# The readout laid into the end of the recurrence, output product and norms by token halves, up projection begun by halves

## The reference

```
hx = modulate(rmsnorm(x, pre_mix_g), sh1, sc1)                 # 1024 tokens; hc likewise, 256 context tokens
q, k, v, o, gates = split(hx @ m_in_w + m_in_b)                # 4 heads, dk 128, dv 256
hxf = chunk_scan(q, k, v, gates_f, state_f)                    # chunks of 128 tokens, first to last
hxb = chunk_scan(reversed q, k, v, gates_b, state_b)           # last to first
h   = hxf + hxb
hn  = h * rsqrt(mean(h*h over each head's 256) + eps) * norm_g
y   = (hn * sigmoid(o)) @ m_out_w                              # the output product
x   = x + g1 * rmsnorm(y, post_mix_g)                          # first norm
hx  = modulate(rmsnorm(x, pre_ffn_g), sh2, sc2)                # second norm
u, g = split(hx @ up_w)                                        # the up projection, 2 x 2816 columns
x   = x + g2 * rmsnorm((silu(dwconv3(g)) * u) @ down_w, post_ffn_g)
```

## Time and profile before

| | |
|---|---|
| timed runs | 2344.55 us median of 3 (2343.93 to 2348.63) |
| profiled execution | 2347.46 us, its span 2345.6 us |
| PE busy | 2157.1 us (92%), 9876 instructions |
| DVE, ACT, POOL busy | 1103.7 (47%), 774.6 (33%), 671.8 (29%) |
| DMA | 245.19 MB, mean 105 GB/s; the SP queue 234.75 MB, 32.5% of 16 engines |
| chain that ended last | PE 41%, issue 38%, DVE 10%, POOL 6% |

### The profile page before, as it was taken

The page is one execution under the profiler, slowest core; times in us unless marked ns, Lnnn a source line. Parts: engine busy times, 40 slices in busy tenths (PEclk is TensorE's granted clock), DMA queues, the critical chain, the costliest instruction groups (busy, mean ns, idle before and its releaser), DMA issues.

```text
span 2345.6 us, 26000 instructions
## 1 busy us (share of the span) xinstructions
PE 2157.1 (92%) x9876; PEld 1785.9 (76%) x9876; DVE 1103.7 (47%) x1039; ACT 774.6 (33%) x884; POOL 671.8 (29%) x308
## 2 busy tenths in 40 slices
PE   5999799997999999999979957979999999999995
PEld 4788687876878787888859946747888888887874
DVE  7689988777333656412236652082222222412124
ACT  4333254564342332122334443232222222302122
POOL 1466455544222221211201124402222222222240
PEclk7999999999999999999989977979999999999997
DMA  9431111221212333356578852121112122123211
GB/s 364 169 128 45 30 59 60 64 68 45 72 59 79 123 90 120 104 172 212 171 200 235 224 200 85 54 72 54 45 45 80 57 77 80 54 72 117 67 59 72
DMA packets 280109, 245.19 MB, mean 105 GB/s; under 512 B 7714, under 2 KB 251523, under 8 KB 280035
## 3 DMA queue, kind: packets, MB, share of 16 engines
q1 hardware_dynamic: 270355, 234.75, 32.5%
q10 hardware_dynamic: 9680, 9.44, 1.2%
HBM read 196.12 MB, written 48.04 MB: 104 GB/s over the span
## 4 chain that ended last, share of the span: by engine, by line
PE 41%; issue 38%; DVE 10%; POOL 6%; DMA 3%; ACT 2%; SPq 0%; POOLq 0%; ACTq 0%; DVEq 0%
PE PS L1372 31%; POOL wl L678 5%; DVE PS L1835 5%; PE PS L1641 1%; PE PS L1649 1%; PE PS L1642 1%; PE PS L1675 1%; PE PS L1528 1%; DVE SCR L1749 1%; DMA B<-rows_d 1%; PE PS L1615 1%; DMA SCR<-in_ctx 1%; PE PS L1635 1%; PE PS L1621 1%; PE PS L1634 1%
## 5 line engine op out<-in xcount | busy, mean ns | idle before, releaser
L1372 PE MATMUL PS<-XH,wh 128*128 128x512 f32 x2448 | 762.9, 393 | 28.9 <-POOL wl L678 18.3
L678 POOL TENSOR_TENSOR wl<-raw,wh 128x1024 fp32r<-128x1024 f32 (+2 forms) x177 | 415.6, 2348 | 1248.0 <-ACT wh L865 1026.1
L1372 PE MATMUL PS<-XL,wh 128*128 128x512 f32 x2448 | 759.1, 391 | 0.0
L1372 PE MATMUL PS<-XH,wl 128*128 128x512 f32 x2448 | 758.4, 391 | 0.0
L1372 PEld LDWEIGHTS PS<-XH,wh 128*128 128x128 f32 x2448 | 460.9, 189 | 133.3 <-POOL wl L678 16.3
L1372 PEld LDWEIGHTS PS<-XL,wh 128*128 128x128 f32 x2448 | 462.5, 189 | 96.9
L1372 PEld LDWEIGHTS PS<-XH,wl 128*128 128x128 f32 x2448 | 462.4, 189 | 96.9
L1835 DVE SCALAR_TENSOR_TENSOR PS<-B,PJ,PS 128x1022 f32<-128x1022 f32 (+7 forms) x197 | 251.1, 1274 | 7.5
L865 ACT ACTIVATE wh<-raw 128x1024 fp32r<-128x1024 f32 (+1 forms) x120 | 125.4, 1045 | 312.4 <-PE PS L1372 245.8
L2246 DVE SCALAR_TENSOR_TENSOR SCR<-SCR,PV 128x1008 f32<-128x1008 f32 x22 | 28.0, 1271 | 256.6 <-ACT SCR L1308 256.6
L939 ACT ACTIVATE wh<-raw 128x1024 fp32r<-128x1024 f32 (+1 forms) x56 | 54.1, 965 | 268.5 <-PE PS L1372 232.8
(11 more groups left out here) (337 smaller groups left out, 2440.7 us busy)
## 6 DMA issues: line engine op xcount, KB each, us to landing
B<-in_ada_w SPq DMA_DIRECT2D x48, 512.0 KB, 6.0
raw<-in_ffn_up_w SPq DMA_DIRECT2D x44, 512.0 KB, 4.1
raw<-in_w_in SPq DMA_DIRECT2D x40, 512.0 KB, 3.8
raw<-in_m_in_w SPq DMA_DIRECT2D x29, 512.0 KB, 5.2
proj_d<-B SPq DMA_DIRECT2D x17, 512.0 KB, 3.0
mod_tiles<-in_mod_w SPq DMA_DIRECT2D x16, 512.0 KB, 13.0
raw<-in_w_out SPq DMA_DIRECT2D x16, 512.0 KB, 4.3
B<-proj_d SPq DMA_DIRECT2D x8, 1024.0 KB, 6.5
```

The source lines that it names most:

```text
L678: tt(wl[slot][:, 0:kc, :], raw[slot][:, 0:kc, :], wh[slot][:, 0:kc, :].bitcast(F32), ALU.subtract).then_inc(lo_done, 1)
L1372: last = mm(ps[:, c:c + step_n], W[:, k, :], Y[:, k, c:c + step_n], start=(seen == 0), stop=(seen == total - 1))
```

## The change

Seven things. (1) `ada_load`: between the weight units, four staging tiles are loaded instead of three from the second group on. (2) In the last round of the linear recurrence a Silu on one element and `ls_evac(7)` come before the casts and the sqrt. (3) The last two of the alternating chunks of the recurrence do no key transposes and no state update; the last eight are unrolled and the readout's parts for four token chunks are called between them (`readout(w)`, w = 0 to 7) on PE, ACT and DVE. Token chunks are taken in the order 3, 4, 2, 5, 1, 6, 0, 7 (`ORDER`), in which both directions finish them, and lie in this order along the token axis from there on. The gate tiles move from ACT's queue to SP's. (4) The output product has 16 units: each weight unit is loaded and cast twice, for tokens 0 to 511 and 512 to 1023 (in the new order); its first two tiles run by quarters. (5) Both norms are done by halves: roots on `[128, 4]`, reciprocals there too, broadcast by a diagonal and one matmul; the sums of the second norm's squares go to POOL. (6) The up projection starts with four tiles by halves (8 units, four weight units loaded twice), then continues as before. (7) The residual is loaded whole before the norms, the output is written in the new order.

```diff
-                for n in range(3 * (U - 3), min(3 * (U - 2), (1 + EARLY) * KD)):
+                for n in range(3 + 4 * (U - 4), min(3 + 4 * (U - 3), (1 + EARLY) * KD)):
                     ada_load(n)
...
# ACT, last round of the linear recurrence
                 if last:
+                    f(spare[:], eps[:], ACT.Silu)
+                    ls_evac(i)
                     hi(ls_unit(i) + 2)
                     for k in range(DVE_HIGH, KD - 2):
                         lru_high(k)
...
             lru_high(KD - 2)
-            ls_evac(KD - 1)
             lru_high(KD - 1)
...
# SP, end of the recurrence
+            def half_unit(t):
+                unit(G5.U + t, (G5.U + t) % 2, cols_of(m_out_w, 0, KD, t % KD * P))
+            def gate_load(n):
+                c = ORDER[n]
+                sp.dma_start(H_GATE[n], proj_d[...][:, :, P * c + CTX:P * (c + 1) + CTX])
+            def read_load(n):
+                c = ORDER[n]
+                for d in range(2):
+                    sp.wait_ge(*at(f"h_out{d}", 16 * (max(c, NT - 1 - c) + 1)))
+                dst = (blocks(H_SUM[n]), H_NORM[n])
+                for d in range(2):
+                    sp.dma_start(dst[d], h_d[d][P * c:P * (c + 1), :].rearrange("p (k t) -> p k t", k=KD))
+            with sp.Fori(0, NT // 2 - 2) as i:          # h_store and chunk_load as before
+            for n in range(4):
+                gate_load(n)
+            for j in range(NT - 4, NT - 2):
+                for d in range(2):
+                    h_store(j, d)
+                    chunk_load(j + NC + 2, d, j % 2)
+                for n in range(2):
+                    read_load(2 * (j - NT // 2) + n)
+            for t in range(2, 4):
+                half_unit(t)
             for j in range(NT - 2, NT):
                 for d in range(2):
                     h_store(j, d)
+            for n in range(4, NT):
+                sp.wait_ge(*at("xl_r", n - 3))
+                read_load(n)                            # n == 4 also waits for all of h_out
+            for n in range(4, NT):
+                gate_load(n)
+            for n, c in enumerate(ORDER):
+                sp.dma_start(B2[:, :, P * n:P * (n + 1)], x2_d[...][:, :, P * c:P * (c + 1)])
+            for t in range(4, 2 * KD):
+                half_unit(t)
+            for u in range(8):
+                unit(G6.U + u, (G6.U + u) % 2, cols_of(up_w, 0, KD, FFN * (1 - u % 2) + P * (u % 4 // 2)))
...
# DVE, called after heads() of each of the last eight
+            def readout(w):
+                if w in (2, 4):
+                    for n in range(2):
+                        read_sum(w - 2 + n)             # waits for h_in
+                if w == 4:
+                    read_norm(0)
+                elif w == 5:
+                    read_norm(1)
+                    read_gate(0)
+                elif w == 6:
+                    read_gate(1)
+                    read_norm(2)
+                    read_norm(3)
+                elif w == 7:
+                    read_gate(2)
+                    read_gate(3)
...
# ACT
+            def readout(w):
+                if w in (3, 5):
+                    for n in range(2):
+                        read_ssq(w - 3 + n)
+                if w == 6:
+                    read_high(0)
+                if w in (4, 6):
+                    read_root(w - 4)
+                if w == 7:
+                    for n in range(1, 4):
+                        read_high(n)
...
# POOL: low parts and sums of squares
+            X_SUMS = {10: (0, 3), 11: (3, 6), 12: (6, KD)}
+            for t in range(2 * KD - 1):
+                half_low(t + 2)
+                y_sum(t)
+                for k in range(*X_SUMS.get(t, (0, 0))):
+                    x_sum(0, k)
...
# PE
+                for n in {5: (0,), 6: (1,), 7: (2, 3)}.get(w, ()):
+                    read_transposes(n)
...
+            for t in range(2, 2 * KD):
+                if t in (3, 5):
+                    for n in range(2):
+                        read_transposes(t + 1 + n)
+                if t == KD:
+                    pe.wait_ge(*at("xl_r", NT))
+                elif t == KD + 1:
+                    half_sums(PS[2], part(ysum_t, 0), event="n2_ps0")
+                elif t == KD + 2:
+                    half_stat("n2", PS[2], part(T[4], 0), 0)
+                elif t == KD + 6:
+                    half_sums(PS[3], part(xsum_t, 0), event="n3_ps0")
+                elif t == KD + 7:
+                    half_stat("n3", PS[3], part(T[4], 1), 0)
+                half_tile(G5, t, PS[b], t // KD)
...
+            half_opening(G6, 0, first, 0, "xl_G6", {3: second_half_sums, 6: second_half_stat})
+            half_tile(G6, 2, PS[2], 0)
+            half_tile(G6, 3, PS[3], 0)
+            half_sums(PS[1][:, HALF:], part(xsum_t, 1), part(xsq_t, 1), event="n3_ps1")
+            half_stat("n3", PS[3], part(T[4], 1), 1)
+            half_opening(G6, 4, first, 1, "xl_G6")
+            half_tile(G6, 6, PS[2], 1)
+            half_tile(G6, 7, PS[3], 1)
+            group(G6_REST, release="x_used_G6")
```

More of the change, by code:

```diff
@@ L372, in recurrence, with is_final @@
             if step:
-                step.done(NT // 2 - 1)
-            for u in range(4):
-                pair(NCH // 2 - 1, u, True, True, u < 3)
+                step.done(NT // 2 - 2)
+            for w in range(8):
+                pair(NCH // 2 - 2 + w // 4, w % 4, True, True, w < 7)
+                if readout:
+                    readout(w)
+        def is_final(x):
+            return isinstance(x, int) and x >= 2 * NCH - 2
         def indices(k, slot, d):
@@ new lines, in _, with first_low @@
+            half_low(2 * KD + 1)
+            def first_low(u):
+                low(G6.U + u, (G6.U + u) % 2)
+            first_low(2)
+            for k in range(3):
+                x_sum(1, k)
+            first_low(3)
+            for k in range(3, 6):
+                x_sum(1, k)
+            first_low(4)
+            x_sum(1, KD - 2)
+            for u in range(5, 9):
+                first_low(u)
+            with pool.Fori(0, KF - 2) as i:
+                for s in range(2):
+                    low(G6.U + 9 + 2 * i + s, (G6.U + 9 + s) % 2)
@@ new lines, in readout, with piece, half_tile @@
+            def readout(w):
+                for n in {5: (0,), 6: (1,), 7: (2, 3)}.get(w, ()):
+                    read_transposes(n)
+            recurrence(pe, transposes, heads, readout=readout)
+            def piece(ps, w, X, k, c, n):
+                for m, (W, Y) in enumerate(((wh[w], XH), (wl[w], XH), (wh[w], XL))):
+                    last = mm(ps[:, c:c + n], W[:, k, :], Y[:, k, c:c + n], start=(k == 0 and m == 0), stop=(k == KD - 1 and m == 2))
+                return last
+            def half_tile(g, t, ps, h):
+                pe.wait_ge(lo_done, g.U + t + 3)
+                for k in range(KD):
+                    last = piece(ps, (g.U + t) % 2, None, k, HALF * h, HALF)
+                last.then_inc(unit_used, 1)
@@ new lines, in half_opening @@
+            def half_opening(g, t, pss, h, ready, between={}):
+                pe.wait_ge(lo_done, g.U + t + 4)
+                for k in range(KD):
+                    if k in between:
+                        between[k]()
+                    pe.wait_ge(*at(ready, KD * h + k + 1))
+                    for s in range(2):
+                        last = piece(pss[s], (g.U + t + s) % 2, None, k, HALF * h, HALF)
+                        if k == KD - 1:
+                            last.then_inc(unit_used, 1)
@@ L1673, in _ @@
                     for k in range(KD):
-                        for n, (W, Y) in enumerate(((wh[w], XH), (wl[w], XH), (wh[w], XL))):
-                            last = mm(ps[:, half * c:half * (c + 1)], W[:, k, :], Y[:, k, half * c:half * (c + 1)],
-                                      start=(k == 0 and n == 0), stop=(k == KD - 1 and n == 2))
+                        last = piece(PS[b], (G5.U + s) % 2, None, k, 2 * P * c, 2 * P)
                     if c == 1:
                         last.then_inc(unit_used, 1)
-            tiles(G5)
```

546 lines of the change are left out of this document (296 added, 250 removed).

## The result

The changed kernel takes 2325.65 us (median of 4 runs, 2322.84 to 2328.7) against 2346.22 (4 runs, 2343.93 to 2348.63): ratio 0.9912, 95% interval 0.9896 to 0.9928, so 21 us faster, give or take 4. The forecast was 2311.5, a gain of 34.4. The profiled execution took 2326.14 us (span 2324.4), 21.2 shorter than that of before, so the two traces hold the whole difference. Beside a row of this part, a line such as L1776 is a line of the kernel that the row comes from.

A forecast was written before the change was run, and what follows sets the result against it. TensorE, busy 92% of the span, was taken as the bound, so only its idle places could give time. Gains of 13 + 9.4 + 12 = 34.4 us from 2347.46 gave 2313.1, set to 2311.5; range 2268 to 2338.

The forecast's parts named there:

- Steps 3 to 5: Readout in the recurrence, output product, norms and first up tiles by halves: together gain 12 us, from -18 to 60.
- Step 1: Conditioning loads by fours: the wait before the first gate matmul goes, 13 us gained (0 to 14).
- Step 2: Last Silu earlier, so the output product after the first recurrent part opens sooner: 9.4 us gained (3 to 11).
- Step 3: Readout in the recurrence: VectorE's sums wait for reads, delaying PE 13 and 10.5 us; output product starts 15 us earlier.
- Rival B: 512-byte pieces move at the long rows' rate, 1.38 us each: 14 us more gain, 2297; chance 0.10.
- Step 4: Output product by halves: a new stall of 18 us (0 to 25) before the fifth weight unit; product ends at 1531.5.
- Step 5: Norms and first up tiles by halves: 69 us from the output product's end to four complete up tiles.
- rival A: No waits in the recurrence or for the fifth unit; output product starts at 1387, total 2268; chance 0.18.
- Rival C: Both early edits give nothing, as PE waits at the same places for something else: 2334; chance 0.15.
- D: Slower: strided or strip pieces take 4.8 us instead of 2.1 in the reworked end, total 2363; chance 0.10.

The follow-up runs named there:

- kernel 1: Only the two early edits (ada loads by fours, last Silu earlier) on the kernel before the change: 2334.26 us against 2350.77.
- kernel 3: Changed kernel with the Silu's table step and the last ls eviction late again: 2330.6 us.
- kernel 5: Changed kernel with the eight residual loads laid between the loads of output weight units 5 to 12: 2309.49 us, ratio 0.9831 to the kernel before.
- kernel 6: Changed kernel with the second norm's fifteen sums of squares moved from GpSimd to VectorE: 2314.35 us, ratio 0.9861 to the kernel before.
- kernel 2: Changed kernel with the ada loads by threes again: 2333.79 us, 0.29% above the changed kernel.
- kernel 4: Changed kernel with VectorE's sums of stored and new h one chunk later in the recurrence: 2312.42 us, ratio 0.9837 to the kernel before.
- kernel 7: Changed kernel with VectorE's sums one chunk later and the residual's loads between the weight units: 2298.52 us, ratio 0.9783 to the kernel before.

## Why the prediction was right, and where it was wrong

Direction held, and the mechanism of the two early edits; the time lies in the range (2268 to 2338), but at the very end of the forecast's own band (2325.65 in 2298 to 2326). The gain was 21.2 us by the profiles instead of 34.4. Steps 3 to 5 failed in their sizes, one by a rate that was misread, one by the time of the matmuls between short waits, and it was luck that the errors had both signs. Its steps, in the order of the sum:

**Step 1, 13 predicted, 11.0 measured.** The 10.6 of the wait came as worked out, down to its release: DVE's last sums end at 140.3 (141.4 predicted). The 2.5 added for the clock came at the place (0.77 and 0.55 in 280:290 and 290:300 before, 1.00 in both after), but this execution lost 2.7 elsewhere; kernels 1 and 3, which did not, have 13.7.

**Step 2, 9.4 predicted, 8.3 by the last stores, some 6 at the second product, 4 at the end.** The wait left is the predicted 2. At the end of the opening, which the last channel blocks set as said, 7.5 are there; what thins it out later was not found.

**Step 3, product's start 15 earlier predicted, 25.5 measured.** The place was right (DVE in order behind reads, first and third sum, PE idle beside it), the sizes were not: DVE waited 7.5 and 4.0 for 13 and 9, PE 7.6 and 5.9. The error is the rate for 512-byte pieces. I had divided GB/s by the DMA share, as if a share of 1 were all that the engines can do. The windows of after show otherwise:

```profile
1290.00:1300.00 10.00, 10.00 (x65) 9.20 (x64) 6.35 (x12) 4.02 (x8) 1.27 (x1) 1.00 1.17 310
1310.00:1320.00 10.00, 5.58 (x41) 4.96 (x39) 2.56 (x3) 0.61 (x1) 1.26 (x1) 0.93 1.11 343
```

The share passes 1 and the rate reaches 343 GB/s: 1.5 to 1.7 us for 512 KB where 2.1 was assumed. Eight residual pieces issued back to back took 14.03, 1.75 each; the gates 2.38. The Trainium skill's rule that I had set aside (DMA: Bandwidth & Descriptors, Specifications: line rate from 512 bytes) is nearer to the 310 to 343 of these windows than my 271, though none of them reached the 368 of the long rows, and the gates at 2.38 were slower than either. Rival B, with 1.38 for all pieces, had the better rate in the recurrence and the worse end. ACT's table loads took 1.28 each and the activation followed within 0.02 (loads at 1339.48 and 1341.10, activations at 1340.78 and 1342.39), so leaving out more was right.

**Step 4, a stall of 18 predicted, 12.0 measured; from there to the product's end 76.5 predicted, 87.3 measured.** The stall's place and cause are shown by kernel 5. The unit was usable 14.1 us sooner than predicted (1421.55 + 19.3 for the early edits = 1440.9, against 1455), mostly because step 3 ended sooner: the first of the last reads went out at 1399.7, counted the same way, and not at 1411, 11.3 sooner. The eight reads took 6.3 us of SP's queue for 11.1, the residual 14.1 for 16.8; against that the gates took 9.6 for 8.4 and the unit itself, from its issue, 11.2 for 7.7. Of the 10.8 that the rest took more, 7.4 are waits behind GpSimd's sums of squares (3.81 + 6.14, where the sum had 2.5; kernel 6 takes most of them away), and the 3.4 left over fit the slow matmuls beside them (1480:1500 at 0.68).

**Step 5, 69 predicted, 82.0 measured** (1508.9, the end of the product's last matmul, to 1590.9). The waits were right in total: 20.2 us in seven (4.94, 2.95, 0.5, 2.63, 1.49, 2.48, 5.18) where the sum had 3.8, 2.8, 0.5, 1.8, 4, 2.2 and 5, though its 4 held PE's sums and broadcast of the last norm too. What failed is the time between them: 61.8 for 48.9. The second halves of the first two tiles took the 13.9 that the sum had with its 3 for the clock (1558.58 to 1572.4). The excess lies in the pieces for which it had the full clock: the first halves of the first two tiles with the sums in them took 16.8 for 12.9 (clock 0.82), the next two half tiles 13.1 for 10.8 (0.87), the last norm's sums and broadcast 4.9 (0.57), the last two half tiles 13.3 for 11.3 (0.86). Over the whole stretch the clock is 0.81, and none of these pieces reaches 1.00 in the mean.

The terms close: 34.4, less 3.1 (steps 1 and 2), plus 14.1, less 10.8 (step 4), less 13.0 (step 5) is 21.6. Steps 3 to 5 gave 2, predicted 12, by errors of both signs. The forecast's rival A had the right view of what was in reach: its product start (1387 without the early edits, 1368 with them) is met by the four kernels with the sums later (1366.7 to 1375.0). Only its stretch after that was too short: 170 us where either form takes 181 to 186.

Rival C falls by kernels 1 to 3; D by all.

## What to carry to other kernels

Work that is laid into another stage enters in-order queues: for each inserted operation ask what stands behind it, and place it where its data have surely landed, here one chunk later for 11 to 18 us. A long burst of loads that is needed late (the residual) goes between those that are needed soon, not ahead of them, for 13 to 19. And when the wait of one engine is replaced by several short ones, count a slow clock in between (0.81 over 81 us here).

## What the runs showed of the hardware

The DMA share of a window is no fraction of what the engines can move: 1.17 at 310 GB/s, 1.11 at 343, 0.97 at 368.

DVE's operations on 128x512, 0.75 us alone, took up to 2.68 beside GpSimd (DVE, then GpSimd, changed kernel):

```profile
1529.93 0.75 DVE L2405 SCALAR_TENSOR_TENSOR B<-B,SC 128x512 f32<-128x512 f32 x1
...
1531.32 2.68 DVE L2405 SCALAR_TENSOR_TENSOR B<-B,SC 128x512 f32<-128x512 f32 x1
```

```profile
1531.10 2.35 POOL L714 TENSOR_TENSOR wl<-raw,wh 128x1024 fp32r<-128x1024 f32 x1 [17.59 <-ACT wh L919]
```

The long one starts 0.22 after GpSimd's operation and ends 0.55 after its end, as if it had stood for all of it. By the Trainium skill (SBUF — State Buffer, SBUF: two separate sides) the two engines share a port pair that one of them holds for a whole instruction (VectorE's with two inputs in SBUF, as here, against a GpSimd operation that reads SBUF); the trace agrees here. It would explain, too, why GpSimd's adds of 128x512 took from 1.3 to 2.3 us; that is not shown.

Single executions of the same code differ by 3 us at 500 us and by 4.9 between the same two waits (16.1 or 21.0 us; clock 1.00 or 0.50 in 1350:1360, kernels 4 and 7), with the same waits of PE before. A difference of a few us between two profiles is to be read from stretches, not from spans.
